# Two transformer blocks on one core: memory keys and values of both layers built in one stage, and low halves split on VectorE from the spread on

## The reference, cut to what matters

```
def _peer(h, w_q, keys, u_tab, v_tab):            # first block, once per layer, by blocks of rows
    q = (hb @ w_q).reshape(n, 8, 2, 128)
    s = einsum('nhpk,pek->nhpe', q, keys)         # scores of 2 x 128 keys per head
    ...                                           # top 16 of each, top 16 of their sums: e, g
    a = gelu(einsum('nhkd,nd->nhk', u_tab[e], hb)) * g
    return einsum('nhk,nhkd->nd', a, v_tab[e])

# between the blocks: x = _rmsnorm(x, final_norm_g)

def second_block(x, mem, ...):
    for i in range(2):
        h = rms_norm(x, norm_mix_w[i])
        mem_n = rms_norm(mem, mem_norm_w[i])
        ...                                       # layer 0: gated delta rule, layer 1: sparse attention
        mo = memory_attention(qm, mem_n, mem_w_kv[i])
        x = x + concatenate([mix, mo], -1) @ w_out[i]
        x = x + conv_glu(rms_norm(x, norm_ffn_w[i]), ...)
    return rms_norm(x, final_norm_w)

def memory_attention(qm, mem_n, w_kv):            # 4 heads of 128
    k, v = split(mem_n @ w_kv)                    # 256 rows x 1024 columns
    p = softmax(einsum('bshd,bmhd->bhsm', qm, k) * 128 ** -0.5)
    return einsum('bhsm,bmhd->bshd', p, v)
```

## Time and profile before

| | us |
|---|---|
| median of 3 runs | 4674.44 (4668.58 to 4679.57) |
| the profiled execution | 4667.18, span 4665.4 |
| experts of layer 0, steps 0 to 71 | 606 to 1554 |
| experts of layer 1, steps 0 to 71 | 2656 to 3209 |
| spread of layer 1 | 2822 to 3083 |
| two norms and the tap load between the blocks | 3568.9 to 3592.5 |
| memory norm and projection, layer 0 | 3851.9 to 3892.7 |
| memory norm and projection, layer 1 | 4336.4 to 4377.3 |

### The profile page before, as it was taken

The page is one execution under the profiler, slowest core; times in us unless marked ns, Lnnn a source line. Parts: engine busy times, 40 slices in busy tenths (PEclk is TensorE's granted clock), DMA queues, the critical chain, the costliest instruction groups (busy, mean ns, idle before and its releaser), DMA issues. The chain is left out here.

```text
span 4665.4 us, 62592 instructions
## 1 busy us (share of the span) xinstructions
PE 4221.3 (90%) x25474; PEld 3635.8 (78%) x25474; DVE 2585.9 (55%) x4989; ACT 1672.7 (36%) x2106; POOL 942.2 (20%) x234
## 2 busy tenths in 40 slices
PE   5899889999999999999779789989998987988798
PEld 4876478888887888888668689988886876977687
DVE  3735368877750244444474489932666654644564
ACT  2333033333333322222245244434444423533443
POOL 1321024333333100000043275553000040000000
PEclk7999989999999999999888899999999988988899
DMA  5421124455548655555333356667886303643264
GB/s 212 157 92 57 70 92 127 136 181 181 181 175 310 223 196 198 189 190 198 113 117 127 138 168 206 222 244 237 288 289 204 120 1 109 190 149 112 95 177 140
DMA packets 453624, 770.80 MB, mean 165 GB/s; under 512 B 20277, under 2 KB 324629, under 8 KB 433081
## 3 DMA queue, kind: packets, MB, share of 16 engines
q1 hardware_dynamic: 452698, 764.69, 49.0%
q10 hardware_dynamic: 640, 2.11, 0.1%
HBM read 663.35 MB, written 103.38 MB: 164 GB/s over the span
## 5 line engine op out<-in xcount | busy, mean ns | idle before, releaser
L1525 POOL TENSOR_TENSOR pr_wlo<-pr_w,pr_whi 128x2048 fp32r<-128x2048 f32 x142 | 668.2, 4706 | 1030.3 <-ACT pr_whi L1636 1030.3
L113 PE MATMUL bank<-hThi_l,pr_whi 128*128 128x512 f32 (+1 forms) x2304 | 789.8, 343 | 37.3 <-POOL pr_wlo L1525 27.5
L113 PE MATMUL bank<-hTlo_l,pr_whi 128*128 128x512 f32 (+1 forms) x2304 | 778.3, 338 | 0.0
L113 PE MATMUL bank<-hThi_l,pr_wlo 128*128 128x512 f32 (+1 forms) x2304 | 778.0, 338 | 0.0
L1636 ACT ACTIVATE pr_whi<-pr_w 128x2048 fp32r<-128x2048 f32 x270 | 515.6, 1910 | 254.1 <-DMA pr_w<-peer_v_in 238.0
L113 PE MATMUL bank<-pr_whi,pr_ahi 128*128 128x512 f32 x1536 | 598.7, 390 | 5.9 <-DVE pr_alo L1800 5.9
L113 PE MATMUL bank<-pr_wlo,pr_ahi 128*128 128x512 f32 x1536 | 598.3, 390 | 0.0
L113 PE MATMUL bank<-pr_whi,pr_alo 128*128 128x512 f32 x1536 | 598.3, 389 | 0.0
L1777 DVE TENSOR_SCALAR pr_hot<-iota,pr_choice 128x128 f32<-128x128 f32 x768 | 455.2, 593 | 105.2 <-PE bank L1573 91.4
L113 PEld LDWEIGHTS bank<-hThi_l,pr_whi 128*128 128x128 f32 x2304 | 440.7, 191 | 88.8 <-POOL pr_wlo L1525 32.0
L113 PEld LDWEIGHTS bank<-hThi_l,pr_wlo 128*128 128x128 f32 x2304 | 440.7, 191 | 45.8
(11 more groups left out here) (515 smaller groups left out, 8105.6 us busy)
## 6 DMA issues: line engine op xcount, KB each, us to landing
pr_w<-peer_u_in SPq DMA_DIRECT2D x128, 1024.0 KB, 5.7
pr_w<-peer_v_in SPq DMA_DIRECT2D x128, 1024.0 KB, 5.0
dense_weights<-pr_buf SPq DMA_DIRECT2D x12, 4096.0 KB, 16.9
gu_w<-ffn_w_up_in SPq DMA_DIRECT2D x88, 512.0 KB, 4.8
mx_w<-w_in_in SPq DMA_DIRECT2D x32, 1024.0 KB, 5.3
expert_scores<-pr_s SPq DMA_DIRECT2D x64, 512.0 KB, 6.7
pr_gs<-expert_scores SPq DMA_DIRECT2D x64, 512.0 KB, 5.9
pr_g<-dense_weights SPq DMA_DIRECT2D x64, 512.0 KB, 7.1
```

Source lines behind the costliest of these rows:

```text
L113: ins = pe.matmul(psum, a, b, start=first and i == 0, stop=last and i == len(terms) - 1)
L1525: pool.tensor_tensor(w_lo[:, n % ring, :, :], wt[:, n % ring, :, :], w_hi[:, s, :, :].bitcast(F32), ALU.subtract).then_inc(lo_ready, 1)
```

## The change

Five edits.

1. `memory_and_norms` is new. One stage takes the place of the norm between the blocks, of the first layer's mix norm and of both layers' memory norms and projections. The memory rows are normalised without a gain; the gain is applied per channel to the transposed tiles, once for each layer, with columns of `cat` as scratch. TensorE makes 16 items (8 weight tiles in three slots), and after the first 8 the transposes of the mix norm. Keys and values of both layers stay in SBUF.
2. The tap load becomes part of the next projection (`early`, `before_follow`), and the memory rows are loaded during the expert phase of layer 1 (step m = 56 of the output phase) into the half of `xrows` that is then free.
3. Layer 0 calls `attend` alone; in layer 1 the 8 memory items stand at the head of the sparse list of 32.
4. In `peer`, GpSimd makes low halves only up to tile `on_pool - 1` (25 in layer 0, 23 in layer 1); VectorE makes the others, one ahead of each step's one-hot groups.
5. In layer 1 the modulation chunks are multiplied 8 steps after the spread instead of 3; they are fetched at the same step as before.

```diff
@@ project
+            for dst, src in early:
+                sp.dma_start(dst, src).then_inc(early_in, 16)
...
             chain = Chain(dve, follow_step)
+            if before_follow:
+                before_follow(dve, chain)
+            if early:
+                dve.wait_ge(early_in, 16 * len(early))
@@ peer
-    ada_from = spread_to + 3
+    on_pool = PH + spread_from + 1
+    lead = 3 if nxt else 8
+    ada_from = spread_to + lead
...
-                    c = ada_after(m + 3)
+                    c = ada_after(m + lead)
...
+                    if m == U - 8 and not nxt:
+                        sp.dma_start(x[:, 0:2, :], K.dram["mem"].rearrange("(t p) d -> p t d", p=P)).then_inc(rows_in, 16)
...
-                for n in range(first_v):
-                    if n + 1 < first_v:
-                        split_lo(n + 1)
+                for n in range(1, on_pool):
+                    split_lo(n)
...
                 def score(n):
-                    if n:
+                    if n >= on_pool:
+                        pe.wait_ge(lo_later, n - on_pool + 1)
+                    elif n:
                         pe.wait_ge(lo_ready, n)
...
+                def split_later(n):
+                    dve.wait_ge(hi_ready, n)
+                    dve.tensor_tensor(w_lo[:, n % ring, :, :], wt[:, n % ring, :, :], w_hi[:, n % slots, :, :].bitcast(F32),
+                                      ALU.subtract).then_inc(lo_later, 1)
+
+                for g in groups_after(spread_from):
+                    make_hots(g)
+                for n in range(on_pool, first_v):
+                    split_later(n)
+                    for g in groups_after(n - PH):
+                        make_hots(g)
@@ memory_and_norms (new; SyncE, TensorE, and the loops of ScalarE and VectorE)
+                def fetch(n):
+                    l, c = divmod(n, 4)
+                    if n >= SLOTS:
+                        sp.wait_ge(ready, 2 * (n - SLOTS) + 2)
...
+                sp.dma_start(chan_gain[:, :, :], K.dram["mem_gain"]).then_inc(gain_in, 16)
+                fetch(0)
+                fetch(1)
...
+                for n in range(2, N):
+                    fetch(n)
+                    if n == 4:
+                        ahead.fetch(sp, first_in, rest_in)
...
+                for g in range(4):
+                    turn(g, rows, scaled).then_inc(turned, 1)
+                for i in range(2 * N):
+                    product(i)
+                    if i == 7:
+                        for g in range(4, 8):
+                            turn(g, rows, x_scaled).then_inc(x_turned, 1)
...
+                for n in range(N):
+                    take(2 * n)
+                    take(2 * n + 1)
...
+                    if n + SLOTS < N:
+                        split_hi(n + SLOTS)
+                    if n == 4:
+                        for g in range(4):
+                            act.wait_ge(x_turned, g + 1)
+                            act.activation(hT[0][:, place(g)[0], place(g)[1]], bank(g), ACT.Copy).then_inc(x_hi, 1)
+                ahead.split_hi(act, first_in, ahead_hi)
...
+                split_lo(0)
+                dve.wait_ge(gain_in, 16)
+                memory(0)
+                shift(1)
+                split_lo(1)
+                memory(1)
...
+                split_lo(3)
+                split_lo(4)
+                split_lo(5)
+                for g in range(4):
+                    at = place(g)
+                    dve.wait_ge(x_hi, g + 1)
+                    dve.tensor_tensor(hT[1][:, at[0], at[1]], bank(g), hT[0][:, at[0], at[1]].bitcast(F32), ALU.subtract).then_inc(x_lo, 1)
+                split_lo(6)
+                split_lo(7)
+                ahead.split_lo(dve, ahead_hi)
@@ second_block, sparse_attention
-                normed(f"m{l}", K.dram["norm_mix_w"][l:l + 1, :], hT, ring.ahead(w_in, [(c, 256) for c in range(0, 768, 256)]))
+                first = ring.ahead(w_in, [(c, 256) for c in range(0, 768, 256)])
+                if l == 0:
+                    memory_and_norms(K, xrows, x, cat, kT, v, hT, first)
+                else:
+                    normed(f"m{l}", K.dram["norm_mix_w"][l:l + 1, :], hT, first)
                 if l % 2 == 0:
-                    gdn_layer(K, l, l // 2, hT, cat, qmT, ring, consts, mem_rows)
+                    gdn_layer(K, l, l // 2, hT, cat, qmT, ring, consts)
+                    attend(K, memory_items(kT[l], v[l], qmT, cat), SCALE)
                 else:
-                    sparse_attention(K, l // 2, hT, cat, qmT, ring, consts, cmp_bias)
-            memory_attention(K, l, mem_rows, qmT, cat, ring)
+                    sparse_attention(K, l // 2, hT, cat, qmT, ring, consts, cmp_bias, kT[l], v[l])
...
-        items = []
+        items = memory_items(kT, v, qmT, cat)
```

More of the change, by code:

```diff
@@ L126, in part_width, with project @@
     return columns if columns <= width else width // P * P
-def project(K, weights, k_tiles, acts, jobs, width=256, ring=3, engine="scalar", lo_on="gpsimd", extra=(), buffers=None, ahead=0, side=None):
+def project(K, weights, k_tiles, acts, jobs, width=256, ring=3, engine="scalar", lo_on="gpsimd", extra=(), buffers=None, ahead=0, side=None, before_follow=None, early=()):
     nc = K.nc
@@ L152, in project @@
     following = any(follows)
-    names = ["psum_ready", "psum_free", "step", "hi_ready", "lo_ready", "follow_step", "followed", "extra_in"] + [f"weights{r}" for r in range(ring)] + list(side.names if side else ())
+    names = ["psum_ready", "psum_free", "step", "hi_ready", "lo_ready", "follow_step", "followed", "extra_in", "early_in"] + [f"weights{r}" for r in range(ring)] + list(side.names if side else ())
     K.uid += 1
@@ L158, in project @@
         first = 1 if ahead and split else 0
-        block, ready, free, step, hi_ready, lo_ready, follow_step, followed, extra_in, *loaded = mem.enter_context(stage(K, *names))
+        block, ready, free, step, hi_ready, lo_ready, follow_step, followed, extra_in, early_in, *loaded = mem.enter_context(stage(K, *names))
         if side:
@@ L1518, in _ @@
                 sp.wait_ge(mod_in, 32)
+                if not nxt:
+                    sp.wait_ge(rows_in, 16)
             @block.gpsimd
@@ L1771, in _, with make_hots @@
                 dve.wait_ge(chosen, pairs)
-                for g in range(n_groups):
+                def make_hots(g):
                     if g >= 2:
@@ L2450, in _, with memory_and_norms @@
                     finish(n)
[L2453 removed]
+def memory_and_norms(K, x, x2, cat, kT, v, hT, ahead):
     nc = K.nc
[L2456 to L2468 removed]
@@ L2472, in gdn_layer, with memory_items @@
+def memory_items(kT, v, qmT, cat):
+    return [(qmT[:, h, t * P:(t + 1) * P], kT[:, h, :], None, [v[:, m, h * P:(h + 1) * P] for m in range(2)],
+             cat[:, t, D + h * P:D + (h + 1) * P], None, False) for h in range(MEM_H) for t in range(2)]
+def gdn_layer(K, l, j, hT, cat, qmT, ring, consts):
     nc = K.nc
@@ L2481, in gdn_layer, with padding @@
             w = sb("w", [P, 3 * GH, 4], conv)
-            load(K, (w[:, :, :], K.dram["gdn_conv_w"][j]), fill=((padded[:, :, 0:3], 0.0),))
+            def padding(dve, chain):
+                chain(dve.memset(padded[:, :, 0:3], 0.0))
             def conv_taps(dve, chain, o):
@@ L2909, in _, with second_block @@
                         dve.tensor_tensor(dst, dst, K.ps[2 * t + c][:, :], ALU.add)
-def second_block(K, x, mem_rows, cmp_bias):
+def second_block(K, xrows, cmp_bias):
     nc = K.nc
+    x = xrows[:, 2:4, :]
+    kT, v = ([K.mem.enter_context(nc.sbuf_tensor(f"ma_{name}{l}", shape, F32)) for l in range(DEPTH)]
+             for name, shape in (("kT", [P, MEM_H, T1]), ("v", [P, 2, MEM_W])))
     for l in range(DEPTH):
@@ L2963, in build @@
         x2 = x[:, 2:4, :]
-        mem_rows, K.tri = sb("mem_rows", [P, 2, D]), sb("tri", [P, P])
-        with nc.sbuf_tensor("mid_gain", [P, D], F32) as gain:
-            norm(K, x2, [0, 1], lambda t: gain[:, :], None, x2, loads=[(gain[:, :], K.dram["final_norm_g"].broadcast_to([P, D]))])
-        second_block(K, x2, mem_rows, cmp_bias)
+        K.tri, K.mem = sb("tri", [P, P]), mem
+        second_block(K, x, cmp_bias)
         with nc.sbuf_tensor("fin_gain", [P, D], F32) as gain, nc.sbuf_tensor("fin_rows", [P, 2, D], F32) as rows:
```

169 lines of the change are left out of this document (147 added, 22 removed).

## The result

The changed kernel takes 4611.8 us (median of 4 runs, 4609.3 to 4613.0), the kernel before 4673.0 beside it: a ratio of 0.9867 (95% interval 0.985 to 0.9884). The forecast was 4623, within 4600 and 4650, and faster. The profiled executions stand 54.2 us apart (4665.4 and 4611.2 us of span), against the forecast sum of 51.6.

The account below looks back on a forecast made before the run. TensorE, busy 90% of the span, bounds the kernel; gains must be its waits or idle stretches. 25.0 + 2.5 + 14.3 + 9.8 = 51.6 off 4667.2, plus 7.3 from profile to median, gives 4623 us (4600 to 4650, 8 in 10).

Parts of the forecast that it names:

- Part A: New stage replacing the norm between the blocks and both memory norms with projections: 80.3 us for 105.3, gain 25.0.
- wait before item 10: In the new stage, TensorE stalls 2.7 us because memory tile 5 lands behind the next projection's 3 MB.
- The second stall: In the new stage before item 12, 4.4 us: tile 6's low half queued on VectorE behind the transposes' low halves.
- The merged list: Layer 1's 8 memory items inside the sparse list cost 12.1 us instead of 14.6: gain 2.5, between 0 and 3.8.
- Layer 0's attention alone is unchanged: Layer 0's attention over memory, still called by itself, was expected to keep its length.
- The memory rows: Their 1 MB load in layer 1's output phase delays weight loads four tiles early by 3 us: taken as 0, at worst 3.
- Part B: Low halves moved to VectorE: layer 1's spread gains 14.3 us, the stretch after it 9.8 (7 to 14).
- Sign (1): Layer 1's spread: one-hot tiles never over 0.4 us, no TensorE wait before its matmuls, 246 us instead of 261.
- sign (2): GpSimd (POOL) busy about 440 us instead of 942, with 94 subtractions of 4.7 gone.
- the stage late: Rival: tiles 3 to 7 of the new stage each 4 us late, stage 100.8 us, kernel 4643; chance 0.10.
- the jam takes all: Rival: store and load jam after the spread cancels the gain there, leaving 14.3, kernel 4633; inside the forecast's 0.75.
- The other side: Rival: GpSimd doesn't cause long one-hots, so VectorE carries 10.3 us a step, costing 73 in layer 1; 4720; chance 0.05.

Follow-up runs that it names:

- pool_spread: The changed kernel, but GpSimd keeps the low halves to the end of the spread and VectorE takes them only after it: 4636.2 us.
- pool_also: The changed kernel, with GpSimd also subtracting constants that nobody reads in every step of the spread, beside VectorE's low halves: 4698.9 us.
- lead3: The changed kernel, with layer 1's modulation chunks used three steps after the spread in place of eight, issued at the same place: 4616.4 us.
- list_apart: The changed kernel, with layer 1's eight memory items in a list of their own behind the sparse one, as before: 4623.0 us.

## Why the prediction was right, and where it was not

**The sign and the sum.** 54.2 us measured between the profiles against 51.6. The four terms of the sum gave 57.7 (27.2, 1.9, 16.5 and 12.1). What had been put at nothing cost 3.5 net: 4.7 in the output phase, 2.0 in layer 0's attention and 0.7 elsewhere, less 3.9 gained by the compressed attention. That the total came so close is in part luck. The medians are 61.2 apart; the 7 between the two figures are that the profiled execution of before was 5.8 us under its median and that of after 1.2 over. So most of the 11 us by which 4623 was too high is the 7.3 that the prediction added to its sum for the distance of one profile from its median, which the changed kernel didn't have.

**Part A.** First product 15.8 us in (forecast 15.9), tail 4.9 (5.0), wait before item 10 3.1 (2.7). The second stall, "a stall of 4.4" before item 12, came for the reason given and was 0.9: tile 6's low half was ready 61.3 us into the stage (forecast 61.9), but item 12 was due only at 60.5 (forecast 57.5). What the step missed is the clock after the first stall. Items 10 and 11 took 9.5 us less the 0.9, so 8.6 in place of 5.7, at a granted clock of 0.69. I had put 1.9 of lost clock behind the second stall and none behind the first; it was 2.9 behind the first. The Trainium skill's rule (TensorE: Matmul & The Clock Gate, HAM oscillation), on which the prediction called the trace of before silent for a wait of 2.7, held for this one of 3.1. "Each time", as the prediction put it, is too much: the eight waits in before's spread, up to 2.6 us long, left the granted clock at 1.00. The slower items then gave VectorE the time that the second stall was to cost. Both errors nearly cancel: 78.1 against 80.3. They need not: in four of the other seven kernels with this same stage (`pool_spread`, `pool_also`, `lead3`, `list_apart`) the wait before item 12 is 1.8 to 2.0 us with the lower clock behind it, which was the forecast's picture, and the stage is 1.5 to 2.1 us longer. A small misreading besides: items come every 2.96 us by the earlier trace rows, not 2.86; items 12 to 15 took 2.95 each.

**The merged list** gave 1.9 (forecast 2.5). **"Layer 0's attention alone is unchanged"** was wrong by 2.0 us. Before, it followed a projection; now it follows the end of the gated-delta part, in which TensorE stands for 9.5 us, and it begins at the lower level of the clock:

```profile
3883.08 2.05 PE L2380 MATMUL bank<-ma_kT,b_qmT 128*128 128x256 f32 x4 [9.48 <-PEq L61]
...
3883.00:3891.00 8.00, 6.95 (x24) 5.06 (x24) 4.29 (x13) 4.16 (x11) 0.00 (x0) 0.58 0.00 0
```

The same stretch before the change began at full clock (four matmuls in 1.10 us in place of 2.05). The projection that was taken away had been its warm-up.

**The early taps** cost nothing that can be seen. **The memory rows**, taken as 0 and "at worst 3", cost some 4.7: the 3 us of 1 MB at 357 GB/s were right, but in the stretch with the fullest queue they came through as a wait, with lost clock behind it in seven of the eight profiles. The ground given, weight loads four tiles early, was the wrong queue: the loads that mattered are the weighted tiles, only two ahead.

**Part B.** The mechanism was right and is now shown from both sides. The spread gained 16.5 us against the 14.3 of the listed waits. The other 2.2 are not waits: TensorE's busy time for the same 2075 matmuls went from 246.4 to 244.2 us. Sign (1) said 246. After the spread 13.2 us of waits against 14, the large one 9.92 against 9.9 and at the step forecast; the gain is 12.1 against 9.8, the waits' difference (23.8 - 13.2 = 10.6) and a shorter stretch of low clock. GpSimd is busy for 506 us where sign (2) said 440; that was a slip, since 440 (94 x 4.7) is what goes from the 942, and 942 - 442 = 500 is what stays.

**The rivals.** Neither "the stage late" nor "the jam takes all" happened. The other side, a VectorE with 10.3 us of work in a step, failed in its premise and not in its arithmetic. `pool_also` is that case: steps of 10.25 us, and slower than before. Its 4698.9 is under the rival's 4720, because the spread cost 65 us more than before's (323.0 against 257.9) in place of 73, and because the 14 us after the spread (117.4 against 131.6) were kept, which the rival had struck out.

## What to carry to other kernels

A VectorE instruction that takes many times its usual length and starts and ends with a GpSimd instruction is being held by it. Look at which instructions are: here one-hots and subtractions were, the top-16 search wasn't. The work on GpSimd then isn't free: it costs VectorE its own length, and moving it to VectorE at half that length unloads both.

A wait in an issuing engine's program delays all that stands behind it. Look for what is fetched earliest with the latest condition, and put it behind the stores and loads that others wait for; then spread large transfers so that the queue isn't full when small ones have to pass.

A stage that is removed takes its side effects along. Here it was the warm clock for the next stage; ask of each removed stretch of matmuls who came after it.

## What had not been expected of the hardware

The compressed attention of layer 1 ran at the lower clock in both kernels that have not got part A (32 small matmuls at a median of 373 ns) and at the higher one in all eleven that have it (262 ns). The first row is of the kernel before, the second of the changed one:

```profile
4271.30:4278.20 6.90, 6.85 (x33) 6.85 (x33) 0.19 (x2) 0.70 (x1) 0.00 (x0) 0.51 0.00 0
```

```profile
4262.00:4266.70 4.70, 4.45 (x33) 4.45 (x34) 0.42 (x4) 0.90 (x1) 0.00 (x0) 0.84 0.02 3
```

Its code is the same. TensorE's wait some 9 us ahead of it was 5.38 and 5.66 us without part A, and 4.74 to 5.01 in the eleven with it. That this half microsecond decides is argued, not shown; it was not tried. It is worth 3.9 us of the result, more than the merged list, and was in no forecast. The transposes ahead of both output projections went the other way (24 matmuls at a median of 273 ns before and of 421 after, 1.2 us each time; the granted clock of layer 0's was 1.00 and is 0.63).
